# Expert weights loaded in pieces of 8 KB for two experts at a time, with the contraction laid out by eights

## The reference, cut to what matters

```python
def _ec_moe(h, w_router, w_gate, w_up, w_down):
    cap = EC_FACTOR * L // N_EXPERTS                 # 2 * 256 / 16 = 32 tokens per expert
    aff = softmax(h @ w_router)
    vals, idx = lax.top_k(jnp.swapaxes(aff, 1, 2), cap)
    xs = h[bidx, idx]
    hid = silu(einsum('becd,edf->becf', xs, w_gate)) * einsum('becd,edf->becf', xs, w_up)
    y = einsum('becf,efd->becd', hid, w_down) * vals[..., None]
    return jnp.zeros_like(h).at[bidx, idx].add(y)
```

## Time and profile before

| | |
|---|---|
| median of 3 runs | 1625.37 us (1621.87 to 1625.46) |
| span of the profiled execution | 1619.0 us (its own time is not on the page; the median is 6.4 us above the span) |
| PE (TensorE) busy | 1377.1 us, 85% of the span |
| DVE (VectorE), ACT (ScalarE), POOL (GpSimd) busy | 611.9, 478.8, 104.1 us |
| moved | 376.08 MB, 232 GB/s over the span |
| chain that ended last | PE 68%, DMA 18%, DVE 6%, SP's queue 5% |

### The profile page before, as it was taken

How to read it: one execution, slowest core, us unless ns; L and a number is a source line. 1 busy time by engine, 2 the same in 40 slices (tenths; PEclk the granted TensorE clock), 3 DMA queues, 4 the chain that set the end, 5 groups by cost and what they waited for, 6 DMA issues and landing times.

```text
span 1619.0 us, 21195 instructions
## 1 busy us (share of the span) xinstructions
PE 1377.1 (85%) x8730; PEld 995.8 (62%) x8730; DVE 611.9 (38%) x848; ACT 478.8 (30%) x698; POOL 104.1 (6%) x99
## 2 busy tenths in 40 slices
PE   5999899786655655655699999999999999999997
PEld 1478665531111101111397899998999988899996
DVE  3225636410100100100447545455444455564544
ACT  2423522310000000000344534444344443343443
POOL 0000011100000000000034000000000045100000
PEclk9999999796767767767799999999999999999999
DMA  8443618989999999999641555655666620256562
GB/s 342 151 117 85 226 42 320 409 322 409 410 410 410 410 410 410 409 410 410 226 143 54 157 181 182 195 170 167 193 185 185 181 89 14 78 153 186 170 205 66
DMA packets 136658, 376.08 MB, mean 232 GB/s; under 512 B 8312, under 2 KB 55849, under 8 KB 136400
## 3 DMA queue, kind: packets, MB, share of 16 engines
q1 hardware_dynamic: 134600, 372.89, 65.0%
q10 hardware_dynamic: 1992, 2.26, 0.4%
HBM read 374.07 MB, written 1.05 MB: 232 GB/s over the span
## 4 chain that ended last, share of the span: by engine, by line
PE 68%; DMA 18%; DVE 6%; SPq 5%; ACT 2%; issue 1%; DVEq 0%; ACTq 0%
PE psum L1738 15%; PE psum L1739 15%; PE psum L1740 15%; DMA ring<-in_w_up 6%; DMA ring<-in_w_down 6%; DMA work<-in_w_gate 5%; SPq L528 5%; PE psum L2025 4%; PE psum L2143 3%; PE psum L2110 2%; PE psum L2123 1%; PE psum L1900 1%; PE psum L2105 1%; PE psum L1759 1%; PE psum L1893 1%
## 5 line engine op out<-in xcount | busy, mean ns | idle before, releaser
L1738 PE MATMUL psum<-parts 128*128 128x256 f32 (+1 forms) x1520 | 466.8, 307 | 3.7 <-DVE parts L1471 1.9
L1739 PE MATMUL psum<-parts 128*128 128x256 f32 (+1 forms) x1520 | 466.1, 307 | 0.0
L1740 PE MATMUL psum<-parts 128*128 128x256 f32 (+1 forms) x1520 | 465.8, 306 | 0.0
L1426 DVE TENSOR_TENSOR parts<-ring,parts 128x1024 fp32r<-128x1024 f32 x232 | 282.5, 1226 | 219.5 <-ACT parts L962 219.5
L962 ACT CAST parts<-ring 128x1024 fp32r<-128x1024 f32 x232 | 241.0, 1047 | 277.1 <-PE psum L1740 242.4
L1738 PEld LDWEIGHTS psum<-parts 128*128 128x128 f32 x1520 | 290.3, 191 | 18.8 <-issue 3.3
L1740 PEld LDWEIGHTS psum<-parts 128*128 128x128 f32 x1520 | 290.3, 191 | 13.3
L1739 PEld LDWEIGHTS psum<-parts 128*128 128x128 f32 x1520 | 290.4, 191 | 12.9
L2025 PE MATMUL psum<-ring,work 128*32 128x512 f32 x512 | 90.6, 846 | 64.8 <-DMA ring<-in_w_up 32.7
L2025 PE MATMUL psum<-work 128*32 128x512 f32 x512 | 85.7, 812 | 41.5 <-DMA work<-in_w_gate 21.7
L952 ACT ACTIVATE work<-psum 128x1024 f32<-128x1024 f32 x4 | 4.1, 1024 | 389.5 <-PE psum L2025 389.5
(11 more groups left out here) (315 smaller groups left out, 1483.4 us busy)
## 6 DMA issues: line engine op xcount, KB each, us to landing
ring<-in_w_qkv_b SPq DMA_DIRECT2D x72, 512.0 KB, 3.7
work<-in_w_gate SPq DMA_DIRECT2D x16, 2048.0 KB, 23.8
ring<-in_w_up SPq DMA_DIRECT2D x16, 2048.0 KB, 24.0
ring<-in_w_ada SPq DMA_DIRECT2D x48, 512.0 KB, 8.5
work<-in_w_down SPq DMA_DIRECT2D x12, 2048.0 KB, 24.0
ring<-in_w_gate SPq DMA_DIRECT2D x44, 512.0 KB, 3.9
ring<-in_w_up SPq DMA_DIRECT2D x44, 512.0 KB, 4.6
ring<-in_w_down SPq DMA_DIRECT2D x44, 512.0 KB, 3.6
```

Source lines behind the costliest of these rows:

```text
L1426: dve.tensor_tensor(part_of(lo_slots, t, n), ring[:, slot_2(t), 0:n], part_of(hi_slots, t, n), ALU.subtract).then_inc(lo_ready, 1)
L1738: pe.matmul(out, lhsT[0], rhs[0], start=start, stop=False, skip_group_check=True)
L1739: pe.matmul(out, lhsT[0], rhs[1], start=False, stop=False, skip_group_check=True)
L1740: return pe.matmul(out, lhsT[1], rhs[0], start=False, stop=stop, skip_group_check=True)
```

## The change

A transfer still has 2 MB, but it holds two neighbouring rows of two experts in place of one row of four. Each partition p now holds the rows 8 p to 8 p + 7 of a matrix; a transfer brings rows 8 p + 2 `pair` and the next (8 KB in one piece) for two experts. Two transfers (`half` 0 and 1) make a pair of slices for all four. Slice k of the contraction is now the rows 8 p + k, so everything that lays out the contraction takes every eighth column: the transposes, the modulation columns, the split of `xn`, the router's weights and the transposes of `hd`.

```diff
-        xn_by_k = [xn[:, t].rearrange("p (k c) -> p k c", k=KD) for t in range(TT)]
+        xn_by_k = [xn[:, t].rearrange("p (c k) -> p k c", k=KD) for t in range(TT)]
...
             def load_quad(expert, q):
-                name, k = (("w_gate", "w_up")[q % 2], q // 2) if q < 2 * KD else ("w_down", q - 2 * KD)
+                both, half = q // 2, q % 2
+                name, pair = (("w_gate", "w_up")[both % 2], both // 2) if both < KD else ("w_down", both - KD)
                 out, full, _ = homes[home_of[q]]
-                sp.dma_start(out, d[name][0, bass.ds(expert, EG), P * k:P * k + P, :].rearrange("j p n -> p j n")).then_inc(full, 16)
+                rows = d[name][0, bass.ds(expert + 2 * half, 2), :, :].rearrange("j (p r) n -> p j (r n)", r=KD)
+                sp.dma_start(out.rearrange("p j n -> p (j n)").rearrange("p (j m) -> p j m", j=2),
+                             rows[:, :, 2 * D * pair:2 * D * pair + 2 * D]).then_inc(full, 16)
...
-            act.dma_start(w_rout, d["w_router"][0].rearrange("(k p) e -> p k e", p=P)).then_inc(route_loaded, 16)
+            act.dma_start(w_rout, d["w_router"][0].rearrange("(p k) e -> p k e", p=P)).then_inc(route_loaded, 16)
...
-            def turn(src, ready, bank=0):
+            def turn(src, ready, bank=0, by_eights=False):
...
-                        ins = pe.transpose(ps[bank + k // 2][:, at:at + P], src[:, t, P * k:P * k + P], ident[:, :])
+                        rows = src[:, t].rearrange("p (c k) -> p k c", k=KD)[:, k, :] if by_eights else src[:, t, P * k:P * k + P]
+                        ins = pe.transpose(ps[bank + k // 2][:, at:at + P], rows, ident[:, :])
...
-                    ins = pe.matmul(ps[MOD_BANK[i]][:, 2 * k:2 * k + 2], modrow[:, P * k:P * k + P], pick_row, start=True, stop=True)
+                    row = modrow[:, P * k:P * k + P] if i < 2 else modrow.rearrange("p (c k) -> p k c", k=KD)[:, k, :]
+                    ins = pe.matmul(ps[MOD_BANK[i]][:, 2 * k:2 * k + 2], row, pick_row, start=True, stop=True)
...
-            turn(xn, xt_ready)
+            turn(xn, xt_ready, by_eights=True)
...
-                def by_expert(bank, lhsT, w, k):
-                    for n in range(2):
-                        for j in range(EG):
-                            rows = slice(CAP * j, CAP * j + CAP)
-                            ins = pe.matmul(ps[bank + n][rows, :], lhsT[:, k, rows], w[:, j, 512 * n:512 * n + 512],
-                                            start=(k == 0), stop=(k == KD - 1))
-                    ins.then_inc(tiles_done, EG)
+                def by_expert(bank, lhsT, pair):
+                    ws = [quad(), quad()]
+                    for k in (2 * pair, 2 * pair + 1):
+                        for n in range(2):
+                            for j in range(EG):
+                                rows = slice(CAP * j, CAP * j + CAP)
+                                w = ws[j // 2][:, 2 * (j % 2) + k % 2, 512 * n:512 * n + 512]
+                                ins = pe.matmul(ps[bank + n][rows, :], lhsT[:, k, rows], w, start=(k == 0), stop=(k == KD - 1))
+                    ins.then_inc(tiles_done, 2 * EG)
...
-                for k in range(KD):
-                    by_expert(0, xs, quad(), k)
-                    by_expert(2, xs, quad(), k)
+                for pair in range(KD // 2):
+                    by_expert(0, xs, pair)
+                    by_expert(2, xs, pair)
```

More of the change, by code:

```diff
@@ L2019, in quad @@
                     return tiles_in
-                def by_expert(bank, lhsT, w, k):
-                    for n in range(2):
-                        for j in range(EG):
-                            rows = slice(CAP * j, CAP * j + CAP)
-                            ins = pe.matmul(ps[bank + n][rows, :], lhsT[:, k, rows], w[:, j, 512 * n:512 * n + 512],
-                                            start=(k == 0), stop=(k == KD - 1))
-                    ins.then_inc(tiles_done, EG)
+                def by_expert(bank, lhsT, pair):
[7 more added lines that the diff above has]
+                    ins.then_inc(tiles_done, 2 * EG)
                 pe.wait_ge(xs_ready, g + 1)
-                for k in range(KD):
-                    by_expert(0, xs, quad(), k)
-                    by_expert(2, xs, quad(), k)
+                for pair in range(KD // 2):
+                    by_expert(0, xs, pair)
+                    by_expert(2, xs, pair)
                 pe.wait_ge(hd_ready, g + 1)
                 for k in range(KD):
-                    ins = pe.transpose(ps[6 + k // 4][:, P * (k % 4):P * (k % 4) + P], hd[:, P * k:P * k + P], ident[:, :])
+                    ins = pe.transpose(ps[6 + k // 4][:, P * (k % 4):P * (k % 4) + P], hd.rearrange("p (c k) -> p k c", k=KD)[:, k, :], ident[:, :])
                 ins.then_inc(hd_turned, 1)
                 pe.wait_ge(hdT_ready, g + 1)
-                for k in range(KD):
-                    by_expert(4, hdT, quad(), k)
+                for pair in range(KD // 2):
+                    by_expert(4, hdT, pair)
                 pe.wait_ge(pick_g_ready, g + 1)
@@ L2287, in laid_out @@
     column(C_GMIX, a["norm_mix_g"][0])
-    column(C_GFFN, a["norm_ffn_g"][0])
+    cols[:, C_GFFN:C_GFFN + KD] = a["norm_ffn_g"][0].reshape(P, KD)
     column(C_MIX2, a["norm_mix_2"].reshape(-1))
@@ L2294, in laid_out @@
     column(C_ADA, a["b_ada"][0])
+    for m in (3, 4):
+        cols[:, C_ADA + KD * m:C_ADA + KD * m + KD] = a["b_ada"][0][D * m:D * m + D].reshape(P, KD)
     column(C_COND, a["c"][0])
```

## The result

| | before | after |
|---|---|---|
| median of the runs, us | 1623.76 (1620.75 to 1628.25) | 1631.37 (1626.49 to 1631.98) |
| ratio, with its 95% interval | 1 | 1.0035 (1.0019 to 1.0052) |
| profiled execution: span, us | 1619.0 | 1630.2 |
| granted TensorE clock, mean | 0.904 | 0.915 |

What follows compares the result with a forecast made beforehand. The prediction took bytes per second in the experts' weight stream to bound the kernel there. Its terms, -12.5 + 1.7 + 2.1 + 1.7 - 0.4 = -7.4 us, took 1625.4 to 1618.0 us, range 1613 to 1628.

Steps and rivals of the forecast that it cites:

- The stream: Experts' weight loads: 8 KB pieces raise the rate from 410 to 422 GB/s over 440 us of transfer, -12.5 us.
- Rivals 1 and 2: Stream stays at 410 GB/s, pair's costs remain, 1630.5 us, chance 0.16; stream at 416 GB/s, 1624.2 us, chance 0.12.
- Rival 3: Cheaper ends: last pair at full clock (+0.7), second block's first load lands early (0); 1614.9 us, chance 0.08.
- The restart: Experts' start: the first place comes back only at the pair's end, at 338.39 not 336.68, +1.7 us.
- The last pair: Experts' end: TensorE has a pair's work behind the last landing, 5.03 us in place of 2.91, +2.1 us.
- What waits for the last places: Second block's first four loads wait for a place now freed at the end of TensorE's experts, +1.7 us.
- The small edits: w_router in 128 pieces, not 1024, -0.4 us; strided transposes of xn taken as 0, with +3.7 as the end.
- They would just be in time: Strided splits of xn before the experts: even twice as long, they would meet TensorE's need at 323.4; no cost.
- Rival 4: Strided reads are slow: TensorE's transposes of xn take twice as long, +3.7, 1621.7 us; chance 0.08.

Runs made afterwards that it cites:

- e1: The change's layout by eights with its strided reads, but loads and products as before (one row of four experts, 4 KB pieces): ratio to before 1.0065.
- e4: The change with slices of 256 rows by twos in place of 1024 by eights, 8 KB pieces dense in HBM, reads with step two: ratio to before 0.9984.
- e9: As e8, with the first two loads of each group also in 4 KB pieces, each worked on and given back alone: ratio to before 0.9936.
- e2: The change, with ScalarE writing the two modulation rows in the order by eights so TensorE reads them without a step: ratio to before 0.9998.
- e3: The change, with the splits of xn reading without a step: ratio to before 1.0017.
- e5: The kernel before with one edit, TensorE's strided read (every eighth column) of the modulation rows: ratio to before 1.0041, +6.6 us.
- e6: The kernel before with one edit, the splits of xn reading every eighth column: ratio to before 1.0018, +2.9 us.
- e8: As e4, with the last two loads of each group as one row of four experts (4 KB), each worked on and given back alone: ratio to before 0.9923.
- r2: The kernel of e4 measured again: ratio to before 0.9969.
- r3: The kernel of e8 measured again: ratio to before 0.9926.
- r1: The change measured once more: ratio to before 1.0030.

## Why the prediction was wrong

- **The stream, -12.5: right.** 422 GB/s from end to end, as one burst of 101 packets had shown. From C (-8.3), with the restart (+1.7) and the last pair (+3.4) taken off, it is -13.4; 86 loads at 4.97 in place of 5.12 us would be -12.9. e1's C, 1.7 below before's with 4 KB pieces, shows how far a column can be trusted. The 3 cycles per packet of the Trainium skill ("DMA: Bandwidth & Descriptors", section "Why small descriptors are slow (HBM only)") give an estimated 1.1%; measured is 2.9%, so here the trace was right to be preferred. Rivals 1 and 2 are out, and so is a cost of 32 KB steps (e1, e4). Rival 3 is out as well: the last pair took 6.34 us, not 3.64.
- **The restart, +1.7: right.** First later load at 355.01, 3.70 us behind the experts' start, before 1.98; e9 undid it. No group end left the queues idle: the slices stay at 421 to 423.
- **The last pair, +2.1: right in kind, too small.** 6.34 us against 2.91 is +3.4. The bounds had held it (+4.4). I took the 5.03 us of an earlier pair, whose granted clock was 0.72 (748.8 to 753.6 us of before); the last pair of after had 0.56. Of the six other profiles with a last pair in one piece two have less (e2 5.06, e3 5.34) and the rest 6.3 to 6.5.
- **What waits for the last places, +1.7: right for that profile.** D grew by 2.1, and L1446 started 10.9 us behind the experts' end, forecast 10.5. But before's own 19.5 held the combining products at a clock of 0.66, in 5.57 us; where they take 3.70 as in the change, D is 17.7 (e5, e6, e8, e9) and the term is nearer 4. I compared against the one execution that I had, and that its number came out is luck.
- **The small edits, -0.4: here it failed.** The sentence "I take 0, with +3.7 (twice as long) as the end" spoke of the 16 transposes of xn. They did not move (3.68). The modulation steps stood in the same list and got no price at all. Their weight loads read with a step (192 ns each before, 333 after), and they are on the path: 3.8 us for the two, **+5.8 us** in A with the lower clock behind them, +6.6 (3.7 to 9.6) measured alone by e5. Nothing in the rows excluded it: two steps of 1.84 us, doubled, are 3.7 us more, and this bound was never written down. The -0.4 itself is half shown: the issue that was held 2.11 us takes 0.49 in after, but the start of the first modulation step moves by 9 us by chance, and no column can show what that is worth.
- **"They would just be in time": here too.** I compared the splits' end with TensorE's need of them at 323.4 and did not ask what else ran beside the longer GpSimd instruction. ScalarE's casts went from 1.99 to 3.96 us, the split from 4.76 to 5.77, it now overlaps VectorE's cast, and this holds the path for some 2.6 us. The wait was new, not longer. Before's trace had the margin:
```profile
316.37 0.17 DVE L1388 CAST work<-work 16x32 f32<-16x32 uint32 x1
```
The split ended 0.23 us ahead of this cast. ScalarE's 1.97 and GpSimd's 1.01 us more put its end 2.75 us behind the cast's start, and the cast took 2.77 us. B grew by 4.8; e3 gives 2.7 of it back. The rest is the router's products, 6.98 us against 4.04 (a clock of 0.50 against 0.91): eleven of the fourteen profiles have 6.98, and the two profiles of the kernel by twos differ in it (4.08 in e4, 6.98 in r2), so this is not shown to be the change's doing.
- **Sum.** The last pair (+1.3) and the tail (+0.4) were a little too cheap, and 5.8 + 2.6 us of strided reads stood at nothing: -7.4 becomes +2.7. The columns have beside it 2.2 more in B (the router's products), 0.8 in E, 0.9 less for the stream, and not the 0.4 of w_router, whose load lies ahead of them: +5.2. The ratios of the two measurements say 5.7 and 4.9.
- **What one profile of before hides.** That profile is of a rare kind: its mean clock is 0.904, and of the 85 executions of before beside the experiments 77 have 0.93 or more, with times no different. e5, whose edit touches neither B nor D, has 36.8 and 17.7 there, 54.5 us in all, where before has 34.7 and 19.5, 54.2. Measured against e5, B is +2.7 and D +3.9, and with A, C and E as they are the sum is 4.9 us in place of 5.2: what was priced too low is then the tail by 2.2, the last pair by 1.3 and the strided reads by 5.8 and 2.7. Whether the lower clock in A is the change's doing stays open.
- **Rival 4** ("Strided reads are slow", 0.08) named a right mechanism, a strided read on TensorE, at the wrong instruction and with under half of the 8.4 us that strided reads cost; it ended at 1621.7, on the good side. The side that became true had 0.16, all of it on the stream.

## What to carry to other kernels

A layout that made transfers longer made other engines' reads strided here: list each reader, and for every one on the path write down twice its time before the gain is believed. For one that only just fits, look at what runs beside and behind it: here the loss of a 0.23 us margin cost some 2.6 us. A step of two columns was nearly free here where eight doubled the modulation steps and ScalarE's casts, so try the smallest interleave that gives the piece size wanted. And large units cost time at the ends of a stream: keep them in the middle and cut the last ones small (e8 and r3 against by twos: 0.6% and 0.4%).

## What the runs showed of the hardware

- A float32 weight load of 128x128 with a step of 8 columns took 333 ns, 192 without, 196 with a step of 2 (the same line in after, before, e4, in windows on the first step). The transposes of xn with a step of 8 took 3.68 us and their weight loads 227 ns in both kernels, at a granted clock of 0.50. It is not that clock which hides a cost: the shortest record of the transposes of hd took 272 ns before and 274 with a step of 8. Why transposes are spared was not tried.
- ScalarE's two casts of 128x1024: 1.99 us without a step, 2.11 with 2, 3.96 with 8. GpSimd's pair: 4.76, 4.87, 5.77. The Trainium skill's "Advanced Engine Details and Errata", section "SBUF Cachelines", has lines of 16 bytes that want two hits each; fp32 read with a step of 2 has two hits, with one of 8 it has one, and ScalarE, GpSimd and the weight loads above agree with it in order, while the transposes do not.
- A VectorE cast of 16x32 took 2.76 to 2.78 us when it met GpSimd's split (after, r1, e1, e2, e6), and 0.17 otherwise; in r2, where the split is 0.1 us longer than before, the cast starts just as it ends:
```profile
316.10 4.87 POOL L680 TENSOR_TENSOR parts<-tokens,parts 128x1024 fp32r<-128x1024 f32 x2 [44.22 <-ACT parts L943]
```
```profile
320.99 0.17 DVE L1391 CAST work<-work 16x32 f32<-16x32 uint32 x1
```
- The same work up to the first modulation step took 250.0 to 259.4 us, and the slower ones had the lower granted clock (mean of 0 to 240 us 0.97 in e8, 0.94 in r3). One profile of each kernel would have told a false story of 6 us.
